# Rounded weights times both halves of x in one 512-column product, in a two-block float32 network in split precision

## The reference, cut to what matters

```python
# first block, per layer
out = jnp.einsum('bsd,de->bse', merged, w_out[layer])
x = _layernorm(DEEPNORM_ALPHA * x + out, ln_g[layer], ln_b[layer])
# second block, per layer
h = layer_norm(ALPHA * h + 0.5 * swiglu(h, ffn1_w_up[l], ffn1_w_down[l]), ...)
mix = hybrid_mixer(h, ...)                 # ends in merged @ w_o
h = layer_norm(ALPHA * h + mix, ...)
h = layer_norm(ALPHA * h + 0.5 * swiglu(h, ffn2_w_up[l], ffn2_w_down[l]), ...)
return h[:, N_META:]
```

## Time and profile before

| what | value |
|---|---|
| median of three runs | 2460.07 us |
| span of the profiled execution (no other time of it is given) | 2461.1 us |
| PE busy | 2406.2 us (98%), 18906 products |
| weight loads (PEld) busy | 2303.5 us (94%), 18906 |
| DVE busy | 1719.8 us (70%), 2565 instructions |
| ACT busy | 1341.3 us (54%), 2355 instructions |
| chain that ended last | PE 78%, DVE 13%, ACT 3%, DMA 2% |
| mean granted clock of TensorE | 0.992 of full |

### The profile page before, as it was taken

One profiled execution on the slowest core, in us unless ns is written; L12 is line 12 of the kernel. 1 busy time (PEld: TensorE's weight loads), 2 busy tenths in 40 slices (PEclk: granted clock), 3 DMA queues, 4 the chain that ended last, 5 costly groups with the idle time before them and its releaser, 6 DMA issues.

```text
span 2461.1 us, 48297 instructions
## 1 busy us (share of the span) xinstructions
PE 2406.2 (98%) x18906; PEld 2303.5 (94%) x18906; DVE 1719.8 (70%) x2565; ACT 1341.3 (54%) x2355; POOL 90.3 (4%) x101
## 2 busy tenths in 40 slices
PE   9999999999999999999999999999999999999998
PEld 8899999999899999999999997899999999789998
DVE  7888677776888867786766566676566656668665
ACT  6788655544688855563444445454444444555443
POOL 0000000000100000000100010010001001001000
PEclk9999999999899999999999999999999999999999
DMA  7444444455344444445455554345545554434553
GB/s 215 141 151 124 152 155 147 145 171 188 103 148 144 135 141 154 138 145 193 141 172 179 168 153 122 106 141 183 167 159 171 171 171 145 132 109 153 189 179 112
DMA packets 397977, 376.08 MB, mean 153 GB/s; under 512 B 27200, under 2 KB 396014, under 8 KB 397694
## 3 DMA queue, kind: packets, MB, share of 16 engines
q1 hardware_dynamic: 397821, 373.94, 48.2%
HBM read 372.84 MB, written 1.05 MB: 152 GB/s over the span
## 4 chain that ended last, share of the span: by engine, by line
PE 78%; DVE 13%; ACT 3%; DVEq 3%; DMA 2%; issue 1%; SPq 0%; ACTq 0%
PE ps L582 22%; PE ps L584 21%; PE ps L583 21%; DVE scratch L1799 3%; DVE w_lo L1576 2%; DVEq L1798 2%; PE ps L804 2%; PE ps L835 1%; PE ps L836 1%; PE ps L837 1%; ACT w_hi L1086 1%; ACT scratch L1086 1%; DVE xT L1701 1%; DMA raw<-in_ffn_w_up 1%; DVE xT L1698 1%
## 5 line engine op out<-in xcount | busy, mean ns | idle before, releaser
L1576 DVE TENSOR_TENSOR w_lo<-raw,w_hi 128x1024 fp32r<-128x1024 f32 x664 | 812.4, 1229 | 421.2 <-ACT w_hi L1086 419.6
L582 PE MATMUL ps<-x_hi,w_hi 128*128 128x256 f32 (+1 forms) x3664 | 1057.6, 289 | 8.7 <-DVE scratch L2018 3.7
L583 PE MATMUL ps<-x_lo,w_hi 128*128 128x256 f32 (+1 forms) x3664 | 1044.4, 285 | 0.0
L584 PE MATMUL ps<-x_hi,w_lo 128*128 128x256 f32 (+1 forms) x3664 | 1041.4, 284 | 0.0
L1086 ACT ACTIVATE w_hi<-raw 128x1024 fp32r<-128x1024 f32 x664 | 697.9, 1056 | 441.5 <-PE ps L584 358.0
L582 PEld LDWEIGHTS ps<-x_hi,w_hi 128*128 128x128 f32 x3664 | 692.7, 189 | 34.6 <-issue 26.9
L583 PEld LDWEIGHTS ps<-x_lo,w_hi 128*128 128x128 f32 x3664 | 693.8, 189 | 2.0
L584 PEld LDWEIGHTS ps<-x_hi,w_lo 128*128 128x128 f32 x3664 | 695.4, 190 | 0.0
L582 PE MATMUL ps<-big_r,w_hi 128*128 128x272 f32 (+1 forms) x832 | 238.9, 287 | 0.0
L584 PE MATMUL ps<-big_r,w_lo 128*128 128x272 f32 (+1 forms) x832 | 238.1, 286 | 0.0
L1086 ACT ACTIVATE scratch<-ps 128x256 f32<-128x256 f32 (+9 forms) x328 | 122.6, 385 | 172.0 <-PE ps L837 77.4
(11 more groups left out here) (304 smaller groups left out, 3095.4 us busy)
## 6 DMA issues: line engine op xcount, KB each, us to landing
raw<-in_w_in SPq DMA_DIRECT2D x184, 512.0 KB, 4.7
raw<-in_ffn_w_up SPq DMA_DIRECT2D x176, 512.0 KB, 4.4
raw<-in_ffn_w_down SPq DMA_DIRECT2D x64, 512.0 KB, 4.3
raw<-in_mix_w_in SPq DMA_DIRECT2D x64, 512.0 KB, 4.6
scratch<-in_w_in SPq DMA_DIRECT2D x40, 512.0 KB, 4.8
raw<-in_w_mem_kv SPq DMA_DIRECT2D x32, 512.0 KB, 4.6
raw<-in_w_br_ssd SPq DMA_DIRECT2D x32, 512.0 KB, 4.1
raw<-in_ffn_w_down SPq DMA_DIRECT2D x32, 384.0 KB, 3.7
```

Of the source, the lines that this page charges most:

```text
L582: mm(out, wh, xh, start=first, stop=False)
L583: mm(out, wh, xl, start=False, stop=False)
L584: return mm(out, wl, xh, start=False, stop=last)
L1576: tt(w_lo[:, p % PARTS, :, :], raw_at(slot_of(Q, p))[:, :, (p % 2) * P:(p % 2 + 1) * P], wh_f[:, p % PARTS, :, :], ALU.subtract).then_inc( ...
```

## The change

Where 256 tokens are added to x, the products on the same rounded weights are issued as one of 512 columns, with both halves of x side by side; the third product stays at 256 columns and accumulates into the first half of the bank. So the bank holds two partial results, and VectorE adds both to x, with a drain between. To give one access pattern to both halves, `x_hi` and `x_lo` become views of one buffer, and `gates` and `big` get a common view. Stages with 272 tokens stay as they were, since 544 columns don't fit a bank.

```diff
-        x_hi = sb("x_hi", [P, KT, TOK2], F32R)
-        x_lo = sb("x_lo", [P, KT, TOK2], F32R)
+        x_both = sb("x_both", [P, 2, KT, TOK2], F32R)
+        x_hi, x_lo = x_both[:, 0, :, :], x_both[:, 1, :, :]
...
+        h_both = gates_big[:, 0:2 * 6144].rearrange("p (h s) -> p h s", h=2)[:, :, 0:FT * TOK2].rearrange("p h (k s) -> p h k s", s=TOK2)
...
+            def wide_passes(out, s, j, x, xj, first, last):
+
+                mm(out[:, 0:2 * SEQ].rearrange("p (h s) -> p h s", h=2), w_hi[:, s, j, :], x[2][:, :, xj, :], start=first, stop=False)
+                return mm(out[:, 0:SEQ], w_lo[:, s, j, :], x[0][:, xj, :], start=False, stop=last)
+
+            def wide_proj(Q, T, k, p, x):
+
+                bank(T, k)
+                split(Q, p)
+                for j in range(KT):
+                    m = wide_passes(ps[k % 2], p % PARTS, j, x, j, j == 0, j == KT - 1)
+                return m.then_inc(gd, 1)
...
                 def project_out(Q, T, NL, x, n, merged, other_bank=0, heads=2):
...
+                    both = n == SEQ
+                    some = wide_passes if both else passes
...
-                            passes(out, o, j, x, j, j == 0, False)
+                            some(out, o, j, x, j, j == 0, False)
...
                     for o in range(heads, KT):
-                        proj(Q, T, o, o, x, n)
+                        if both:
+                            wide_proj(Q, T, o, o, x)
+                        else:
+                            proj(Q, T, o, o, x, n)
...
+                hidden = [h[:, :, 0:size] for h in (h_hi, h_lo)] + [h_both[:, :, :, 0:size]]
+                down, to = (wide_passes, 2 * SEQ) if size == SEQ else (passes, size)
...
-                                m = passes(ps[o][:, 0:size], p % PARTS, j, [h[:, :, 0:size] for h in hidden], k, k == 0, k == FT - 1)
+                                m = down(ps[o][:, 0:to], p % PARTS, j, hidden, k, k == 0, k == FT - 1)
...
-                c, p = slice(TOK2 - n, TOK2), (third if third and o == 2 else ps[o % 2])[:, 0:n]
+                c, of = slice(TOK2 - n, TOK2), third if third and o == 2 else ps[o % 2]
+                p = of[:, 0:n]
                 if o < SUB:
-                    stt(xT[:, o, c], xT[:, o, c], scale, p, ALU.mult, ALU.add).then_inc(gf[o % 2], 1)
+                    m = stt(xT[:, o, c], xT[:, o, c], scale, p, ALU.mult, ALU.add)
                 else:
-                    tt(xT[:, o, c], xT[:, o, c], p, ALU.add).then_inc(gf[o % 2], 1)
+                    m = tt(xT[:, o, c], xT[:, o, c], p, ALU.add)
+                if n == SEQ:
+                    v.drain()
+                    m = tt(xT[:, o, c], xT[:, o, c], of[:, SEQ:2 * SEQ], ALU.add)
+                m.then_inc(gf[o % 2], 1)
```

More of the change, by code:

```diff
@@ L180, in build @@
         xT = sb("xT", [P, KT, TOK2])
-        x_hi = sb("x_hi", [P, KT, TOK2], F32R)
-        x_lo = sb("x_lo", [P, KT, TOK2], F32R)
+        x_both = sb("x_both", [P, 2, KT, TOK2], F32R)
+        x_hi, x_lo = x_both[:, 0, :, :], x_both[:, 1, :, :]
         mem_hi = sb("mem_hi", [P, KT, SEQ], F32R)
         mem_lo = sb("mem_lo", [P, KT, SEQ], F32R)
-        gates, gates_r = overlaid("gates", [P, 6144])
+        gates_at = -(-nc.sbuf_base // 32) * 32
+        gates = sb("gates", [P, 6144])
         big_at = -(-nc.sbuf_base // 32) * 32
-        big, big_r = overlaid("big", [P, 8192])
+        big = sb("big", [P, 8192])
+        assert big_at == gates_at + 4 * 6144
+        gates_big = nc.alloc_sbuf_tensor_at("gates_big_r", [P, 6144 + 8192], F32R, offset=gates_at)
+        gates_r, big_r = gates_big[:, 0:6144], gates_big[:, 6144:6144 + 8192]
         cum_rows = nc.alloc_sbuf_tensor_at("cum_rows", [P, 2 * SEQ], F32R, offset=big_at + 4 * 7168)
@@ L594, in proj @@
                 return m.then_inc(gd, 1)
-            x1 = (x_hi[:, :, META:TOK2], x_lo[:, :, META:TOK2])
+            x1 = (x_hi[:, :, META:TOK2], x_lo[:, :, META:TOK2], x_both[:, :, :, META:TOK2])
             x2 = (x_hi, x_lo)
             mem = (mem_hi, mem_lo)
-            y1, y2, hidden = (y_hi, y_lo), (y2_hi, y2_lo), (h_hi, h_lo)
+            y1, y2 = (y_hi, y_lo), (y2_hi, y2_lo)
             def first_three(Q, T, x, ready, n):
@@ L832, in token_tile @@
                         for j in range(KT):
-                            xh, xl = [v[:, j, t * P:(t + 1) * P] for v in x]
+                            xh, xl = [v[:, j, t * P:(t + 1) * P] for v in x[0:2]]
                             wh, wl = w_hi[:, s:s + 2, j, :], w_lo[:, s:s + 2, j, :]
@@ L937, in project_out @@
                     pe.wait_ge(S["merged_ready"], merged + 3)
-                    outs = [(ps[0], ps[1], ps[6])[o][:, 0:n] for o in range(heads)]
+                    both = n == SEQ
+                    outs = [(ps[0], ps[1], ps[6])[o] if both else (ps[0], ps[1], ps[6])[o][:, 0:n] for o in range(heads)]
+                    some = wide_passes if both else passes
                     for o, out in enumerate(outs):
@@ L947, in project_out @@
                         for j in range(KT - 2, KT):
-                            m = passes(out, o, j, x, j, False, j == KT - 1)
+                            m = some(out, o, j, x, j, False, j == KT - 1)
                         m.then_inc(gd, 1)
                     for o in range(heads, KT):
-                        proj(Q, T, o, o, x, n)
+                        if both:
+                            wide_proj(Q, T, o, o, x)
+                        else:
+                            proj(Q, T, o, o, x, n)
                         if o == 4:
```

## The result

The changed kernel takes 2466.06 us (median of 11 runs, 2463.51 to 2468.63) against 2460.07 for the kernel before in the same job (11 runs, 2456.06 to 2462.11). The ratio is 1.0024, 95% interval [1.0016, 1.0033]: 6.0 us slower, 3.9 to 8.1. The forecast was 2463.3 (2459.5 to 2467.0). The sign and the range held. The forecast's own narrower range (2461.5 to 2465, chance 0.58) did not hold, nor did the likeliest case, "not to be told from no change" (up to 2465.0): the loss is 0.24%.

The account below looks back on a forecast made before the run. TensorE was taken as busy 98% of the span, but VectorE as the bound in the first block's layer-1 output projection. 1.75 + 2.5 + 1.05 - 2.1 = +3.2 us on 2460.07 gave 2463.3 us, range 2459.5 to 2467.

Parts of the forecast that it names:

- not to be told from no change: Whole kernel: a measured time between 2455.2 and 2465.0 us, given chance 0.68.
- rival 1: Merging gives nothing because the wide product costs two narrow ones; +5.6 us, 2465.7; chance 0.11.
- rival 2: New TensorE waits lower the clock; one drop more makes 2464.8 us, two 2466.3; chance 0.12.
- A: Output projection, layer 0 of the first block: second additions lose 1.75 us.
- C: Output projection, second block, layer 1: most extra additions vanish in VectorE's gaps; 1.05 us lost.
- D: Last down projection: VectorE idles, 176 mergings gain 2.1 us, bounds 0 and 4.2.
- Rival 3: VectorE's added additions fall into its waiting time, so only TensorE's 4.4 us count; 2455.7 us; chance 0.05.
- B: Output projection, layer 1 of the first block: VectorE's extra additions lose 2.5 us, mergings hidden inside the wait.
- 0.50 us a tile: VectorE's price per tile for a drain and second addition, 4.0 us a stage; bounds 0.33 and 0.67.
- I take 12 ns: TensorE's gain per merging of two 256-column products into one of 512; 4.4 us over 368, bounds 0 and 9.
- The slack behind tile 7: Time between tile 7's freed result and TensorE's use of it, subtracted from the loss: 0.25, 0.15 and 0.3 us.
- The gap before the second addition in B: VectorE's wait for TensorE, a gap of 0.30 us that the first addition's extra 0.50 fills.
- the 0.26 us by which the first tile comes earlier: In B, TensorE brings the first tile 0.26 us earlier, through 22 mergings.

Follow-up runs that it names:

- e3: Kernel before, narrow products kept, plus a drain and an unused second addition per tile in the same four stages; 2467.52 us, ratio 1.0028.
- e2: Changed kernel without the drain and second addition, so the remainder product is made but never added to x; 2457.26 us, ratio 0.9991.
- e4: Changed kernel without the drain, its second addition written to scratch from another input so it depends on nothing; 2462.87 us, ratio 1.0012.
- e1: Changed kernel with wide products and second additions only in the last down projection; 2459.17 us against 2460.30 for the kernel before, ratio 0.9998.
- e5: Kernel before with idle products ahead of each layer norm at widths from 128 to 512 columns, one per stage; one execution, 2463.03 us beside 2459.79.
- e8: Kernel before with idle products in eight patterns: 512 columns contiguous or in two pieces, alone or alternating with 256, some accumulating; one execution, 2453.96 us.
- e7: Changed kernel with drain and second addition for tiles 4 to 7 only; one execution, 2459.43 us beside 2459.79.
- e6: Changed kernel with drain and second addition for tiles 0 to 3 only; one execution, 2461.41 us beside 2459.79.
- e9: e1 with each block's rounded part of h next to its remainder, making the 512 columns contiguous; 2457.72 us against 2460.76 for the kernel before, 0.9987.
- e10: The same kernel as e8, timed over 10 runs; 2455.44 us against 2460.71 for the kernel before, ratio 0.9982.
- e12: e9 with the eight idle-product patterns of e8; 2454.11 us against 2460.69 for the kernel before, ratio 0.9972.
- e11: e9 with 15 idle products of 512 columns in place of 30 of 256; 2457.35 us against 2460.71 for the kernel before, ratio 0.9981.

## Why the prediction was right and wrong

The mechanism that set the sign was right: VectorE pays for each second addition in three stages and TensorE gains in the fourth. The sizes were not, and the measured 2466.06 lies in the stated range only because the rivals had widened it. By the number alone rival 1 (2465.7) and two drops of the clock in rival 2 (2466.3) come closest. Neither happened, so that is chance.

- **The bound.** Right: VectorE sets the end in A to C, TensorE in D. e3 shows it without the mergings, e2 without the additions. Rival 3 (the additions are covered) is out: of 4.0 us a stage 0.7 was covered in B (3.30 lost) and 2.2 in C.
- **0.50 us a tile.** Right: start to start 0.49 to 0.50 in all four stages, 0.33 of it the addition and 0.17 the drain (e4).
- **"I take 12 ns" for a merging.** Wrong size. From e1's D it is 5.5 ns, from the pair's pitch 4.4 to 5.0. D gave 1.0 us, not 2.1. The pitch of like products (e5) does not carry over to wide and narrow ones in turn (e8). The truth lies between my 12 ns and rival 1's zero. The formula of the Trainium skill, "TensorE: Matmul & The Clock Gate", section "Back-to-back issue gap", would give 2.5 ns a merging, 0.9 us for the 368, an estimate; measured, 368 x 4.4 ns make 1.6 us. The prediction left out that this section gives the formula for a product by itself and says that it counts too little for narrow products in a stream in which each brings weights. So 118.6 against 109.2 does not speak against the page, and its 2.5 ns are not what these products show: e5 has 12 to 13 ns of fixed time each, and most of that is lost again in the mixed sequence (e8).
- **The slack behind tile 7, 0.25 in B, 0.15 in A, 0.3 in C.** Wrong: there was nearly none. I read it from the start of a piece of the chain (1211.50), which is the time from which the path runs through the instruction, not its start. TensorE in order of time in the kernel before has the second pair at 1211.33, 0.09 behind the freed result:

```profile
1211.33 0.65 PE L638 MATMUL ps<-xT,const 128*128 128x256 f32 x2
```

  After waits 0.40 at this place in all three stages, and e7 shows that it does not come with the first four tiles. In B tile 7's first addition starts 2.80 us later than before, counted from the stage's first event, and the reciprocal 3.30: the last 0.5 arrives whole. Missing: 0.25 us in B, up to that much in the others.
- **The gap before the second addition in B and the 0.26 us by which the first tile comes earlier.** Wrong by the merging's size: the first tile came 0.07 earlier (it ends after 20 mergings, not 22; 20 x 4.4 ns = 0.09), so 0.2 more arrives. e6 has 1.8 arriving where I had 1.4.
- **VectorE's own gap.** In B, after and e3 have 0.44 us on VectorE before it adds the first four tiles together (before has 0.09), for which no wait is shown:

```profile
1201.76 0.69 DVE L1695 TENSOR_TENSOR scratch<-xT 128x512 f32<-128x512 f32 x1 [0.44 <-issue]
```

  e6 has none there (the addition at 1199.49, this at 1200.01), and still its first four additions cost 2.0. VectorE waits later instead, for TensorE at tile 4:

```profile
1205.10 0.42 DVE L1685 TENSOR_TENSOR xT<-xT,ps 128x256 f32<-128x256 f32 x1 [0.44 <-PE ps L594]
```

  Counted from the stage's first event, tile 4's addition starts at 14.53 us in e6 and in after, and at 12.67 in before: 1.86 later, where 1.4 was forecast. So the gap does not make the difference. TensorE, late by its waits for a bank (0.5) and for the partial sum (0.5 in e6), brings tile 4 no sooner. The forecast followed VectorE alone through the first four tiles and missed this.
- **Stage C: 1.05 expected, 1.83 measured.** Besides the slack and the merging, one wait was not foreseen, that of TensorE at tile 2:

```profile
2231.45 0.50 PE L593 MATMUL ps<-x_both,w_hi 128*128 128x512 f32 x1 [0.38 <-DVE xT L1688]
```

  The text ahead of the prediction says that this call has `heads=1`; that is a misreading. The positional 1 is `other_bank`, and `heads` is 2: tiles 0 and 1 share the waits for the merged input, end 0.7 us apart, and tile 2 needs the bank of tile 0 at once, which is now held 0.50 longer. e6 puts a limit on what this can cost: the first four additions together make C 0.5 longer than e2.
- **Stage A: 1.75 expected, 1.8 measured.** The number is luck. I let the loss run over the weight transfer of the earlier trace rows; after's chain has no transfer there and runs over VectorE, as in B. Against before's executions without the late transfer A lost 2.8 us.
- **The clock (rival 2).** Not it: after's profile has less time at 1.2 GHz than before's. But before's profiled execution was a long one, and so the profiles differ by less (3.2 us, by chance exactly the sum that I had forecast) than the medians (6.0). The agreement of the two 3.2 is no support for my sum. The price of one drop was also misread: behind stage B the products have 272 columns, so 32 would run in 4 us and not 34, which makes 1.25 us and not 1.5. And 2461.1 is a span, not a time, so "1.0 us above the median" compares two different measures; the forecast does not hang on it.

In all: A +1.75 forecast and +1.8 measured (+2.8 against the form of before without the late transfer), B +2.5 and +3.30, C +1.05 and +1.83, D -2.1 and -0.97; +3.2 and +5.9 (+6.9). All the errors of the sum point the same way. So the case with the right mechanism, put at "same" with most of its chance, came out just beyond that bound.

## What to carry to other kernels

A product saved on the busiest engine is worth its fixed part only, and that has to be measured in the sequence in which it stands: here 4 to 6 ns out of 119, where like products in a row promised 13. A second pass over a bank on the engine that frees it costs its whole length, drain included, in each stage where that engine is on the path; look at the stage, not at the 70% of the span. In this kernel the trade holds only where VectorE idles, as in the last down projection, which gets 0.7 to 1.0 us shorter (e1, e9). And slack is read from the start of the instruction in order of time, never from a piece of the chain; two versions are compared by stages between events of their own, and a gain of some microseconds by medians of many executions.

## What the runs showed that I had not expected

- The 512-column product starts 227 ns ahead of its like. In turn with narrow ones the next starts after 230, or after 235 to 237 when the wide one reads two far pieces or both accumulate (e8, e10); but in e12 two of these patterns have 230 to 232.
- The idle products of e10, fewer and wider, made the kernel 5.3 us faster though they last as long (15 x 227 = 3.4 us against 30 x 119 = 3.6). With the wide ones alone e11 was no faster than e9. In the profiles the second block's first feed-forward differs in its transfer. The DMA engines' share and GB/s in 40 slices of 1205 to 1236, and the queues, before:

```profile
DMA  6000799940000000000000000003999700049994
GB/s 202 0 0 0 95 370 361 370 147 25 17 0 0 0 0 0 0 0 0 0 0 0 0 0 0 0 0 34 316 362 362 238 21 24 17 87 375 382 379 130
...
q8 instruction: 2, 0.03, 0.7%
```

  and e11:

```profile
DMA  9000289980000000000000000001699910027998
GB/s 351 28 0 0 53 260 371 386 288 5 0 0 0 0 0 0 0 21 0 0 0 0 0 0 0 0 0 17 177 373 382 365 40 0 0 44 254 382 387 283
...
q8 instruction: 1, 0.02, 0.2%
```

  Before, the transfer has a tail of 2 us at 17 to 24 GB/s (slices 33 to 35); e11's has none. Instruction transfers take 0.7% of the engines' time there and 0.2% in e11, so that an instruction fetch in the way of the transfer would fit. This is only argued, and no run separates it.
- After a wait of 2.0 us or more at that place, five of six profiles (before, e1, e3, e4, e9) have a granted clock of 0.91 over 1225 to 1245, part of it at 1.2 GHz, and after has 1.00; with waits of 0 to 1.9 us all eight have 1.00. So the late transfer often costs more than its wait, but not in every execution.
